# Expert mixer: tokens stationary and weights moving 512 wide, context rows in plain fp32 in four column groups at the end of each chunk

## What is computed

```
cap = EC_CAPACITY_FACTOR * n // N_EXPERTS        # 128 latent, 32 context
g, idx = lax.top_k(aff, cap)
xs = jax.vmap(lambda xb, ib: xb[ib])(x, idx)
hcur = jax.nn.silu(jnp.einsum('becd,edf->becf', xs, w_gate)) * jnp.einsum('becd,edf->becf', xs, w_up)
ys = jnp.einsum('becf,efd->becd', hcur, w_down) * g[..., None].astype(x.dtype)
```

## Time and profile before

| | us |
|---|---|
| median of 3 runs | 3937.78 (3931.60 to 3941.98) |
| profiled execution, span | 3935.3 |
| all before the experts' first matmul | 2176.4 |
| experts, first to last matmul | 1681.6, which is 105.1 for each of 16 |
| after the last matmul | 77.3 |

### The profile page before, as it was taken

One profiled execution on the slowest core, in us unless ns is written; L12 is line 12 of the kernel. 1 busy time (PEld: TensorE's weight loads), 2 busy tenths in 40 slices (PEclk: granted clock), 3 DMA queues, 4 the chain that ended last, 5 costly groups with the idle time before them and its releaser, 6 DMA issues. The chain is left out here.

```text
span 3935.3 us, 63550 instructions
## 1 busy us (share of the span) xinstructions
PE 3696.5 (94%) x22946; PEld 3327.2 (85%) x22946; DVE 2454.8 (62%) x4641; ACT 1774.0 (45%) x2654; POOL 470.9 (12%) x517
## 2 busy tenths in 40 slices
PE   5899999999999999999995999999999999999992
PEld 3799999999888888888875898888888888888981
DVE  5755555555566666332227677777777787777774
ACT  4601111111277776311106556666666666565553
POOL 0000000000264644010101000000000000000000
PEclk8999999999999999999997999999999999999996
DMA  9533434443655645646426687888778878788886
GB/s 377 168 130 130 137 124 137 136 139 125 184 173 165 189 141 169 260 142 219 142 83 267 227 259 258 265 258 271 260 258 262 270 256 260 258 266 260 262 257 247
DMA packets 556531, 825.31 MB, mean 210 GB/s; under 512 B 24320, under 2 KB 426144, under 8 KB 544672
## 3 DMA queue, kind: packets, MB, share of 16 engines
q1 hardware_dynamic: 532384, 702.27, 53.9%
q0 software_dynamic: 24064, 121.93, 9.5%
HBM read 717.18 MB, written 108.00 MB: 210 GB/s over the span
## 5 line engine op out<-in xcount | busy, mean ns | idle before, releaser
L2183 DVE TENSOR_TENSOR e_wlo<-e_raw,e_whi 128x1024 fp32r<-128x1024 f32 x768 | 905.2, 1220 | 331.9 <-ACT e_whi L2102 328.6
L2320 PE MATMUL ps<-e_xs,e_whi 128*128 128x320 f32 x4096 | 1056.4, 344 | 10.9 <-DVE e_xs L2197 6.9
L2320 PE MATMUL ps<-e_xs,e_wlo 128*128 128x160 f32 x4096 | 935.2, 238 | 0.0
L2102 ACT ACTIVATE e_whi<-e_raw 128x1024 fp32r<-128x1024 f32 x768 | 765.8, 1048 | 292.0 <-DMA e_raw<-in_w_up 132.2
L2320 PEld LDWEIGHTS ps<-e_xs,e_wlo 128*128 128x128 f32 x4096 | 771.0, 191 | 0.7
L2320 PEld LDWEIGHTS ps<-e_xs,e_whi 128*128 128x128 f32 x4096 | 753.7, 188 | 15.7 <-issue 7.3
L2338 PE MATMUL ps<-e_whi,e_h 128*128 128x512 f32 x1024 | 403.9, 394 | 1.9 <-DVE e_h L2223 1.9
L543 PE MATMUL ps<-hhi,p_whi 128*128 128x428 f32 (+1 forms) x1536 | 381.8, 357 | 8.6 <-DVE p_wlo L475 8.6
L493 DVE SCALAR_TENSOR_TENSOR p_acc<-p_modraw,cT,p_acc 128x256 f32<-128x256 f32 x960 | 386.6, 480 | 0.4 <-DMA p_modraw<-in_w_mod 0.4
L543 PE MATMUL ps<-hlo,p_whi 128*128 128x428 f32 (+1 forms) x1536 | 381.8, 357 | 0.0
L543 PE MATMUL ps<-hhi,p_wlo 128*128 128x428 f32 (+1 forms) x1536 | 380.1, 356 | 0.0
(11 more groups left out here) (256 smaller groups left out, 5246.8 us busy)
## 6 DMA issues: line engine op xcount, KB each, us to landing
e_raw<-in_w_gate SPq DMA_DIRECT2D x64, 2048.0 KB, 8.2
e_raw<-in_w_up SPq DMA_DIRECT2D x64, 2048.0 KB, 8.1
e_raw<-in_w_down SPq DMA_DIRECT2D x64, 2048.0 KB, 8.1
p_modraw<-in_w_mod SPq DMA_DIRECT2D x128, 512.0 KB, 3.5
m_raw<-in_w_mod SPq DMA_DIRECT2D x16, 2048.0 KB, 13.2
p_raw<-in_w_in SPq DMA_DIRECT2D x64, 512.0 KB, 4.8
o_raw<-in_w_out SPq DMA_DIRECT2D x16, 2048.0 KB, 9.3
projT<-p_out_st POOLq DMA_DIRECT2D x30, 640.0 KB, 3.7
```

The source lines that it names most:

```text
L2102: nc.scalar.activation(piece(whi, c, q), piece(raw, c, q), ACT.Copy).then_inc(w_hi_made, 1)
L2183: nc.vector.tensor_tensor(piece(wlo, c, q), piece(raw, c, q), piece(whi, c, q).bitcast(F32), ALU.subtract).then_inc(w_lo_made, 1)
L2320: last = nc.tensor.matmul(bank[:, 0:cols], w[:, s, at:at + P], xs[:, k, 0:cols], start=(k == 0 and w is whi), stop=(k == KD - 1 and w is whi))
```

## The change

The diff turns the product of gate and up round and cuts the context tokens out of the split arithmetic.

- A gate-and-up chunk is now 4 blocks of 128 rows (`GU_KB`) by 512 columns of gate and 512 of up, loaded by two transfers of 1 MB (`load_gate_and_up`). A down chunk is 2 blocks of 128 rows by all 2,048 columns, also two transfers. There are still 12 chunks of 2 MB.
- Latent tokens are stationary everywhere and weights move 512 wide: 24 fp32r matmuls in each chunk (`latent`).
- Context tokens are multiplied in plain fp32 straight from `raw`, in four column groups of 32 (`context`), after the latent matmuls of the same chunk. So PE is now a reader of `raw`, and the load of chunk c waits for `ctx_used` of chunk c-2 as well as for its lo parts.
- The hidden rows come out of PSUM with tokens on partitions, so PE turns them back (`turn_h`), twice for each expert. PSUM banks alternate between even and odd experts.
- The gathered rows have a buffer of their own (`rows_in`), so the gather no longer waits for the scatter; context results are scattered as quarter rows.

```diff
@@ load of a chunk
-                sp.wait_ge(w_lo_made, e * EP + c * NP + NP)
-                sp.dma_start(raw[:, c % 2, :].rearrange("p (k n) -> p k n", k=kb),
-                             w[ds(e, 1), :, col:col + width].rearrange("a (k p) n -> p (a k) n", p=P)
-                             ).then_inc(w_loaded[c % 2], 16)
+                sp.wait_ge(w_lo_made, e * EP + (c - 1) * NP)
+                sp.wait_ge(ctx_used, e * NCH + (c - 1))
+                slot, landed = raw[:, c % 2, :], w_loaded[c % 2]
+                if c < UP:
+                    load_gate_and_up(sp, v, slot, landed, slice(e, e + 1), c // NGU, c % NGU)
+                else:
+                    for k in range(DKB):
+                        at = ((c - UP) * DKB + k) * P
+                        sp.dma_start(slot[:, k * D:k * D + D],
+                                     v["w_down"][e:e + 1, at:at + P, :].rearrange("a p n -> p (a n)")
+                                     ).then_inc(landed, 16)
@@ PE, context rows
+                pe.wait_ge(w_loaded[c % 2], e * LOADS + (c // 2) * 32 + 32)
...
+                if c < UP:
+                    j, i = divmod(c, NGU)
+                    steps = [(xc[:, i * GU_KB + k, :], k * FE, i * GU_KB + k) for k in range(GU_KB)]
+                    bank, width, of = CTX_UP[j], HW, KD
+                else:
+                    i = c - UP
+                    steps = [(hc[:, i * DKB + k, :], k * D, i * DKB + k) for k in range(DKB)]
+                    bank, width, of = CBANK, QD, KF
+                for x, at, k in steps:
+                    for d in range(QUARTERS):
+                        last = nc.tensor.matmul(ps[d * QW:d * QW + QW, bank, 0:width], x,
+                                                raw[:, c % 2, at + d * width:at + d * width + width],
+                                                start=(k == 0), stop=(k == of - 1))
+                last.then_inc(ctx_used, 1)
@@ PE, latent rows
+                for q in range(NP):
...
+                    pe.wait_ge(w_lo_made, e * EP + c * NP + q + 1)
+                    for n, bank in enumerate(banks):
+                        f = slice(q * PW + n * HF, q * PW + n * HF + HF)
+                        for i, (x, w) in enumerate(((hi, whi), (hi, wlo), (lo, whi))):
+                            last = nc.tensor.matmul(ps[:, bank, :], x, w[:, c % 2, f], start=(k == 0 and i == 0),
+                                                    stop=(k == of - 1 and i == 2))
+                    last.then_inc(piece_used, 1)
@@ PE, one expert
+                for c in range(NCH):
+                    latent(e, odd, c)
+                    context(e, c)
+                    if c in (NGU, UP):
+                        turn_h(e, odd, c // NGU - 1)
+                    if c >= UP and not last:
+                        turn_xs(e + 1, c - UP)
@@ POOL, one expert
+                pool.wait_ge(gathered, e * 16 + 16)
+                pool.wait_ge(xs_turned, e * NGR + NGR)
+                gather(e + 1)
+                pool.wait_ge(scattered, e * 32 + FIRST)
+                add_to_y(e)
```

More of the change, by code:

```diff
@@ L1668, in _ @@
                 sp.dma_start(yt[t][:], y_d[t * P:t * P + P, :]).then_inc(y_in[t % FT], 16)
[L1669 to L1672, removed]
+            for c in range(2):
+                load_gate_and_up(sp, v, raw[:, c, :], w_loaded[c], slice(0, 1), 0, c)
         @block.gpsimd
@@ L2047, in _ @@
+            for e in range(E):
+                for c in range(0 if e else 2, NCH):
                     load_w(e, c)
@@ L2166, in _ @@
-            make_hi(0, 0, range(NP))
-            for groups in TURNS:
-                modulate_xs(0, groups)
-                xs_high(0, groups)
-            ctx_high(0)
-            with act.Fori(0, E - 1) as e:
-                expert(e)
-            expert(E - 1, True)
+                        act.wait_ge(w_loaded[c % 2], e * LOADS + (c // 2) * 32 + 32)
+                    act.wait_ge(piece_used, e * EP + c * NP + q + 1)
+                    f = slice(q * PW, q * PW + PW)
+                    nc.scalar.activation(whi[:, c % 2, f], raw[:, c % 2, f], ACT.Copy).then_inc(w_hi_made, 1)
@@ new lines, in make_xs @@
+            def make_xs(n, r, bank=XBANK):
+                act.wait_ge(xs_turned, n * NGR + r + 1)
+                if not (isinstance(n, int) and n * NGR + r < 2):
+                    act.wait_ge(xs_made, n * NGR + r - 1)
+                for i in range(KG):
+                    k = r * KG + i
+                    last = nc.scalar.activation(tmp[:, r % 2, i, :], ps[:, bank, i * CAP_L:i * CAP_L + CAP_L],
+                                                ACT.Identity, bias=addT[:, 0, k:k + 1], scale=mulT[:, 0, k:k + 1])
+                last.then_inc(xs_step, 1)
+                act.wait_ge(xs_step, 2 * (n * NGR + r) + 1)
+                nc.scalar.activation(xhi[:, r * KG:r * KG + KG, :], tmp[:, r % 2], ACT.Copy).then_inc(xs_step, 1)
@@ L2175, in _ @@
+            make_hi(0, 0)
+            copy_xc(0)
+            for r in range(NGR - 1):
+                make_xs(0, r, FIRST_XBANKS[r])
+            with act.Fori(0, E // 2 - 1) as i:
+                expert(i * 2, 0)
+                expert(i * 2 + 1, 1)
+            expert(E - 2, 0)
+            expert(E - 1, 1, True)
         @block.vector
         def _(dve):
-            nc.vector.memset(gsum[:, 0, :], 0.0).then_inc(piece_used, SLOTS)
-            nc.vector.memset(gsum[:, 1, :], 0.0).then_inc(w_lo_made, SLOTS)
@@ L2278, in expert @@
-                scale_ys(e, ND - 1, last)
-            make_lo(0, 0, range(NP))
-            build_xs(0, range(NGR))
-            ctx_lo(0)
-            with dve.Fori(0, E - 1) as e:
-                expert(e)
-            expert(E - 1, True)
+                    if c < NCH - 1:
+                        make_lo(e, c + 1)
+                    elif not last:
+                        make_lo(e + 1, 0)
+                scale_ctx(e)
+                for d in range(QUARTERS):
+                    scale_ys(e, odd, d)
@@ L2287, in _, with turn_xs @@
+            make_lo(0, 0)
+            for r in range(NGR - 1):
+                xs_low(0, r)
+            with dve.Fori(0, E // 2 - 1) as i:
+                expert(i * 2, 0)
+                expert(i * 2 + 1, 1)
+            expert(E - 2, 0)
+            expert(E - 1, 1, True)
         @block.tensor
         def _(pe):
[L2290 removed]
+            def turn_xs(n, r, bank=XBANK):
                 pe.wait_ge(gathered, n * 16 + 16)
[L2292 to L2299 removed]
@@ L2348, in _ @@
-            turn_xs(0, range(NGR), None)
-            with pe.Fori(0, E - 1) as e:
-                expert(e)
-            expert(E - 1, True)
+                if not (isinstance(n, int) and n == 0):
+                    pe.wait_ge(xs_step, 2 * (n * NGR + r) - 1)
+                for i in range(KG):
+                    k = r * KG + i
+                    last = nc.tensor.transpose(ps[:, bank, i * CAP_L:i * CAP_L + CAP_L], rows_in[:, k * P:k * P + P],
+                                               ident[:])
@@ new lines, in expert @@
+            def expert(e, odd, last=False):
+                for c in range(NCH):
+                    latent(e, odd, c)
+                    context(e, c)
+                    if c in (NGU, UP):
+                        turn_h(e, odd, c // NGU - 1)
+                    if c >= UP and not last:
+                        turn_xs(e + 1, c - UP)
+            for r in range(NGR):
+                turn_xs(0, r, FIRST_XBANKS[r])
+            with pe.Fori(0, E // 2 - 1) as i:
+                expert(i * 2, 0)
+                expert(i * 2 + 1, 1)
```

529 lines of the change are left out of this document (241 added, 288 removed).

## The result

| | before | after |
|---|---|---|
| median, us | 3935.84 (4 runs) | 4181.58 (4169.39 to 4186.15, 4 runs) |
| ratio | | 1.062, 95% interval 1.060 to 1.0639 |
| profiled span | 3935.3 | 4167.4 |
| experts, first to last matmul | 1681.6 | 1925.5, which is 120.3 per expert |

The change costs 6.2%. The prediction was 4032 with a range to 4180: the direction and the ring are right, the size is 150 us short.

What follows compares the result with a forecast made beforehand. PE bounds the kernel before; afterwards a ring of load and PE work would. Sixteen experts at 111.2 us give 1779 against 1681.6 (+97.6); with start and end +94 on span 3935.3, median 2.5 higher: 4032 us, range 3925 to 4180.

Steps and rivals of the forecast that it cites:

- the ring: Experts' stage: load, hi, lo, latent and context matmuls, then reload of the same raw slot; 18.15 us per two chunks.
- Scatter and gather ... 2.3 us per expert: Experts' stage: loads sharing DMA engines with scatter and gather lengthen; one falls on each ring, adding 2.3 us per expert.
- I cost it at nothing: Gather freed from the scatter: moves the same bytes together without lessening them, so no cost was counted.
- rival 3: Experts' stage: PE's new waits lower its clock; a tenth of columns slow gives 4102 us, a fifth 4170; chance 0.13.
- W = 7.3 us of PE per chunk: PE's work per chunk: 5.42 us latent matmuls, 1.71 context rows, 0.15 for weight loads and changes of form.
- rival 2: Context rows: four groups don't overlap with 32 stationary columns; 4195 us (chance 0.10), or 4640 if one after another (0.02).
- this change of form: PE switching between stationary widths: a drain costs at most 0.16 us, twice a chunk; time at most +31 us.
- X: Time in which a raw slot is not on PE, from context rows' end to the next latent matmuls: 10.85 us.
- PE's own saving: Experts' stage: if PE stayed the bound, its shorter work would save 14 us per expert, 225 in all.
- Wider rows and two transfers: Weight loads: no gain taken for wider rows, at most -101 us; splitting into two transfers costs up to +43 us.
- Rival 1: Weight loads take under 7.2 us from issue to hi part, so the time falls to 3894 us; chance 0.15.
- The start: First chunk of the experts' stage waits for a quarter of the turned rows, not all; 5 of 6.92 idle us regained.

Runs made afterwards that it cites:

- the last version: Changed kernel with context rows first, gather behind the scatter, and DVE scaling context results before the next expert's first lo parts: 3812.8 us, ratio 0.9692 to the kernel before.

## Why the prediction was short

The ring was foreseen, and most of its parts. This is the ring of the even chunks (six turns per expert, experts 3 to 15), added up from the timelines of SP, ACT, DVE and PE, beside the prediction's own terms, in us per expert:

| | predicted | measured |
|---|---|---|
| end of the context rows to issue | 2.0 | 0.7 |
| six loads, issue to hi part | 48.9 + 2.3 for scatter and gather | 53.5; that of chunk 2 is 14.3 of it |
| hi part to lo part | 6.5 | 6.5 |
| lo part to PE's first matmul | 7.7 | 10.4 |
| PE's work | 43.8 | 49.5, some 4 of it by the lower clock |
| sum | 111.2 | 120.6 |

The difference, 9.4 us for 16 experts, is the 150 us that were missing.

- **"Scatter and gather ... 2.3 us per expert": this is the step that failed.** I read the price in two loads of one expert and gave each ring one. The load of chunk 2 took 14.3 us where an undisturbed one of gate and up takes 8.0, so the term is 6.3 and not 2.3. Leaving out the scatter gives 104 us, where the sum had 37 for scatter and gather together: 5.0 us per expert in the even loads and 1.3 in PE's work. The two loads that I read were short cases even before: of the same two places, those of experts 3 to 15 landed after 11.5 and 10.6 us on average, and the longest after 13.4. PE had covered them then.
- **"I cost it at nothing"**, of the freed gather: the same step. It brings the transfers together beside the loads of chunks 2 and 3; parting them again gives 49 us.
- **The clock** was rival 3 and stood at nothing in the sum. It came, at 0.94 for the stage, and stretches the latent parts of the even chunks by some 4 us per expert, as much as the term above lacks. Part of it follows from the long loads, as the run without the scatter shows. No run shows what the clock alone costs.
- **W = 7.3 us of PE per chunk.** Nearly right: latent starts 0.23 apart, context rows 1.92, a chunk 7.5 where PE never waits. The four groups overlap with 32 stationary columns as with 2; rival 2 is refuted. Context rows begin 0.32 us after the last latent start where the usual distance is 0.23; so this change of form costs 0.1 us, less than the 0.16 that I had as a bound.
- **The ring.** Right in its place: context rows first, and context rows from another tile, each remove it and give 316 and 338 us. In the turn shown X was 10.37 for 10.85. Not in the sum was that a chunk whose lo part is ready finds PE still busy with the other ring: 10.4 us from lo part to PE for 7.7. Of PE's own saving, forecast as 225 us if PE stayed the bound, about half is there once the ring is gone: 122 us in the last version.
- **Wider rows and two transfers.** Taken as nothing, which was a little too high: in the middle of experts 3 to 15 the median from issue to hi part is 7.85 us for gate and up (8.03 before) and 7.4 for down (8.2 before). The estimate of 6.8 us from the Trainium skill (DMA: Bandwidth & Descriptors, the anatomy of one DMA) does not agree with the trace after either; the shortest of these loads took 7.2. Rival 1 needed under 7.2 for all of them.
- **The start** came 12 us earlier, not 5. Of this, 5.4 us are there already before PE and ACT make the gate rows in `router` (ACT scales the rows ahead of them from 2107.6 on, for 2113.0), and the lead is the same behind them; where it comes from stays open. The other 7 us stand against the 5 of the forecast.

## What to carry to other kernels

When an instruction becomes the last reader of a buffer that a transfer refills, follow the ring: reader, issue, landing, the steps to the next reader, and compare its length over the number of slots with the bound of today. The price of a transfer that was hidden is not to be read from one typical case in the old trace; take the longest at least, if the change uncovers it. Here even that one, 13.4 us to landing, was under the 14.3 that followed. And put the reader that needs the raw data at the head of its stage, where it frees the buffer while the rest still works.

## What the runs showed of the hardware

- With the scatter that adds into memory under way, the DMA engines were busy 0.97 of the time at 252 GB/s; in the five microseconds after it, with the gather still on its way, 1.03 at 410. The loads of chunks 2 and 3 took 14.3 and 13.3 us with the scatter and 8.8 and 8.7 without: it cost each of them 4.6 to 5.5 us, where its 160 rows of 8 KB come to 3.2 us at 410 GB/s.
- PE ran at 1.2 GHz for some 3 us after a wait of 5.7 us, though it was busy 83% of the stage. After the wait of 1.85 us its 24 matmuls started every 0.23 us (3011.93 to 3017.31), but other waits of that length went otherwise: of 49 chunks behind a wait of 1.8 to 2.9 us, 22 had latent parts of 7.1 to 7.4 us and the others of 5.7 to 5.8.
- Two transfers of 1 MB in place of one of 2 MB, with rows of 2 KB for 1 KB, took 7.85 us from issue to hi part for 8.03 (medians); with rows of 8 KB for 2 KB they took 7.4 for 8.2.
- 16 plain fp32 matmuls of 256 columns in four column groups took 1.92 us with 32 stationary columns, as they had taken 1.91 with 2.
